# Twelve wide slabs multiplied without splitting, x loaded behind six modulation units, six warming products per sum

## What is computed

```
mod = c_act @ ada_w[l] + ada_b[l]
shift, scl, gate_res = split(mod, 3)
h = rms(x, norm_g[l]) * (1 + scl) + shift
z = h @ w_in            # even layer: 6144 columns u, q, k, v, g; odd layer: more
y = concat(two branches made of z)
x = x + gate_res * ((y * silu(g)) @ w_out[l])
```

## Time and profile before

| | |
|---|---|
| median of 3 runs | 1003.92 us (1001.75 to 1004.96) |
| the profiled execution: its time | 1002.58 us |
| its span, first to last instruction | 1000.8 us |
| mean granted TensorE clock | 0.993 of full speed |
| PE, DVE, ACT busy | 96%, 82%, 42% |
| DMA | 261.31 MB, mean 261 GB/s |
| chain that ended last | PE 85%, DVE 7%, DMA 3%, ACT 2%, issue 2% |

### The profile page before, as it was taken

One profiled execution on the slowest core, in us unless ns is written; L12 is line 12 of the kernel. 1 busy time (PEld: TensorE's weight loads), 2 busy tenths in 40 slices (PEclk: granted clock), 3 DMA queues, 4 the chain that ended last, 5 costly groups with the idle time before them and its releaser, 6 DMA issues.

```text
span 1000.8 us, 19413 instructions
## 1 busy us (share of the span) xinstructions
PE 962.8 (96%) x7328; PEld 931.3 (93%) x7328; DVE 821.0 (82%) x1242; ACT 423.6 (42%) x687; POOL 46.2 (5%) x62
## 2 busy tenths in 40 slices
PE   3799979999999999999999999999999999999998
PEld 3689879999999999999999999999999999998887
DVE  5767887986999779888778899888999996888964
ACT  2210135434555444433435444444446555743331
POOL 1000000020110000000000000000010100000000
PEclk9999899999999999999999999999999999999999
DMA  9999979888876878999957655544445455587962
GB/s 363 396 390 359 348 239 339 326 300 332 303 282 230 288 261 299 339 350 351 327 180 273 229 182 193 187 142 154 155 162 174 159 187 191 195 314 272 375 218 81
DMA packets 71525, 261.31 MB, mean 261 GB/s; under 512 B 7952, under 2 KB 8592, under 8 KB 71200
## 3 DMA queue, kind: packets, MB, share of 16 engines
q1 hardware_dynamic: 66240, 240.90, 66.4%
q10 hardware_dynamic: 2880, 10.49, 2.7%
q0 software_dynamic: 2336, 8.98, 2.5%
HBM read 256.07 MB, written 4.19 MB: 260 GB/s over the span
## 4 chain that ended last, share of the span: by engine, by line
PE 85%; DVE 7%; DMA 3%; ACT 2%; issue 2%; SPq 0%; ACTq 0%; DVEq 0%
PE bank L752 17%; PE bank L753 16%; PE bank L754 16%; PE bank L808 6%; PE bank L773 6%; PE bank L890 3%; PE bank L892 3%; PE bank L893 3%; PE bank L771 3%; DVE wlo L1110 3%; PE bank L821 2%; DVE acc L1120 2%; PE bank L842 2%; PE bank L739 1%; DMA X<-xT 1%
## 5 line engine op out<-in xcount | busy, mean ns | idle before, releaser
L434 ACT ACTIVATE whi<-raw 128x1024 fp32r<-128x1024 f32 x264 | 278.2, 1060 | 419.7 <-PE bank L754 296.6
L1110 DVE TENSOR_TENSOR wlo<-raw,whi 128x1024 fp32r<-128x1024 f32 x264 | 319.7, 1223 | 85.3 <-ACT whi L434 84.1
L752 PE MATMUL bank<-hhi,whi 128*128 128x256 f32 x1168 | 337.1, 289 | 2.2 <-ACT T L664 0.9
L753 PE MATMUL bank<-hlo,whi 128*128 128x256 f32 x1168 | 330.4, 283 | 0.0
L754 PE MATMUL bank<-hhi,wlo 128*128 128x256 f32 x1168 | 330.3, 283 | 0.0
L752 PEld LDWEIGHTS bank<-hhi,whi 128*128 128x128 f32 x1168 | 223.9, 192 | 5.5 <-issue 3.8
L753 PEld LDWEIGHTS bank<-hlo,whi 128*128 128x128 f32 x1168 | 224.0, 192 | 0.1
L754 PEld LDWEIGHTS bank<-hhi,wlo 128*128 128x128 f32 x1168 | 223.9, 192 | 0.0
L1120 DVE SCALAR_TENSOR_TENSOR acc<-ada,cact,acc 128x1024 f32<-128x1024 f32 x152 | 195.2, 1284 | 19.1 <-DMA ada<-ada_units 7.4
L1330 DVE SCALAR_TENSOR_TENSOR Y<-U,par,Y 128x256 f32<-128x256 f32 x240 | 98.5, 478 | 0.0
L773 PE MATMUL bank<-both_g,whi 128*128 128x512 f32 x256 | 89.9, 398 | 0.1
(11 more groups left out here) (186 smaller groups left out, 1314.8 us busy)
## 6 DMA issues: line engine op xcount, KB each, us to landing
raw<-w_slabs SPq DMA_DIRECT2D x262, 512.0 KB, 4.7
ada<-ada_units SPq DMA_DIRECT2D x160, 512.0 KB, 6.7
raw<-w_slabs ACTq DMA_DIRECT2D x20, 512.0 KB, 7.5
V<-ada_units SPq DMA_DIRECT2D x16, 512.0 KB, 11.5
Y<-ada_units SPq DMA_DIRECT2D x16, 512.0 KB, 10.9
X<-xT SPq DMA_DIRECT2D x1, 2048.0 KB, 12.4
x_dram<-X POOLq DMA_DIRECT2D x4, 512.0 KB, 6.3
outT<-X POOLq DMA_DIRECT2D x3, 512.0 KB, 6.1
```

The lines of the kernel that those rows point to most:

```text
L434: act.activation(whi[:, slot], raw[:, slot], ACT.Copy).then_inc(hi_done, 1)
L752: mm(out, whi[:, s, k, :], ahi[:, c, :], start=(c == 0), stop=False)
L753: mm(out, whi[:, s, k, :], alo[:, c, :], start=False, stop=False)
L1110: dve.tensor_tensor(wlo[:, s], raw[:, s], whi[:, s].bitcast(F32), ALU.subtract)\
```

## The change

- `UNSPLIT` becomes 12: chunks 12 to 15 go through `unsplit_chunk` too. `hi` and `lo` of slabs 9, 10 and 11 are gone, and `full_h` makes h for chunks 12 to 15.
- Before a sum there is no warming. After each sum (and after the spread) come 6 products of `keep_warm`, also before chunk 14.
- The spread of the root comes after the sum of piece 0. DVE adds all 16 units of piece 0 before `rsqrt`; ACT loads its table for the root early (`warm(ACT.Sqrt)`) and issues slabs 0 and 1 behind `root`.
- x is issued behind six units instead of four.
- Slab 12 has no place in `raw`: SP loads it into Y (`load_spare`) when all 64 units are added. Behind it SP issues units 64 and 65, slab 14, slab 13, and units 66 to 69.
- DVE's work between the half units of piece 3 is in another order.

```diff
-UNSPLIT = 9
+UNSPLIT = WIDE[0]
...
+        def spare_half(half):
+            return Y[:, 4 * half:4 * half + 4, :].rearrange("p a (b n) -> p (a b) n", n=P)
+
+        def load_spare(eng):
+            eng.wait_ge(ada_done, FIRST + 4)
+            for half in range(2):
+                eng.dma_start(spare_half(half), w_slabs[UNSPLIT:UNSPLIT + 1, :, 8 * half:8 * half + 8, :]
+                              .rearrange("a p k n -> p (a k) n")).then_inc(y_in[half], 16)
+
         def load_slab(eng, w, t):
             for half in range(2):
                 slot = half_slot(w, half)
-                if w >= UNSPLIT + 2:
+                if w == UNSPLIT + 2:
+                    eng.wait_ge(pe_half, 2 * (w - 2) + half + 1)
+                    eng.sem_inc(raw_in[slot], 16)
+                elif w > UNSPLIT:
                     eng.wait_ge(lo_done, 2 * now(w, t) + half + 1)
+                    if w == UNSPLIT + 1:
+                        eng.wait_ge(pe_half, 2 * w + half + 1)
                 elif w >= 2:
                     eng.wait_ge(pe_half, 2 * w + half + 1)
...
-            load_units(0, 4, None)
+            load_units(0, 6, None)
             sp.dma_start(X[:], xT).then_inc(x_in, 16)
-            load_units(4, FIRST - 4, None)
+            load_units(6, FIRST - 6, None)
+            load_slab(sp, UNSPLIT - 2, None)
+            load_slab(sp, UNSPLIT - 1, None)
+            load_spare(sp)
+            load_units(*units_at(10), None)
+            load_slab(sp, UNSPLIT + 2, None)
             load_slab(sp, UNSPLIT + 1, None)
-            load_slab(sp, UNSPLIT + 2, None)
+            load_units(*units_at(11), None)
+            load_units(*units_at(12), None)
...
+            act.wait_ge(const, 1)
+            warm(ACT.Sqrt)
             act.wait_ge(x_in, 16)
             for j in range(KC):
                 square_x(j, j)
+            root(0, QT)
+            act.wait_ge(ada_in[unit_slot(12)], 16 * unit_uses(12, None))
             load_slab(act, 0, None)
             load_slab(act, 1, None)
-            root(0, QT)
...
-            hi(9, None)
-            upper_h(0, range(12, 14))
-            hi(10, None)
-            upper_h(0, range(14, 16))
-            hi(11, None)
+            full_h(range(12, 14))
+            full_h(range(14, 16))
             hi(12, None)
...
-            spread_token(0)
 
             for p in range(3):
                 if p:
-                    pe.wait_ge(ada_done, UNITS * p + 12 + 4)
-                    keep_warm(14, M)
                     pe.wait_ge(ada_done, UNITS * p + 14 + 4)
-                    keep_warm(10, M)
                 reduce_piece(p)
+                if p == 0:
+                    spread_token(0)
+                keep_warm(6, M)
                 for c in range(GROUP * p, GROUP * (p + 1)):
...
-            wide_chunk(0, U0, 12)
-            wide_chunk(0, U0, 13)
+            unsplit_chunk(12)
+            unsplit_chunk(13)
             pe.wait_ge(ada_done, UNITS * 4 + 4)
             for j in range(4, HC):
                 reduce_part(3, j)
-            wide_chunk(0, U0, 14)
-            wide_chunk(0, U0, 15)
+            keep_warm(6, M)
+            unsplit_chunk(14)
+            unsplit_chunk(15)
...
-            add_units(0, 14, None)
+            add_units(0, 16, None)
             dve.wait_ge(stat_done, KC)
             rsqrt(0, QT, M[:, 0:QT], D_MODEL)
             token_diag()
-            add_units(14, 2, None)
...
-            half_units(56, 4)
-            lo(9, None)
+            half_units(56, 2)
             first_half()
-            half_units(60, 2)
-            lo(10, None)
-            half_units(62, 2)
+            half_units(58, 6)
             keep_piece(3, first=4)
             make_gain(0, 3, h0=1)
             make_h(0, range(14, 16))
-            lo(11, None)
```

More of the change, by code:

```diff
@@ L160, in build @@
         raw_in = [sem(f"raw_in{i}") for i in range(4)]
+        y_in = [sem(f"y_in{i}") for i in range(2)]
         ada_in = [sem(f"ada_in{i}") for i in range(8)]
@@ L301, in step @@
                 load_units(*units_at(w), t)
-            for w0, w1 in ((10, 34), (34, 48), (48, 62), (62, 72), (72, 110), (110, 125), (125, 131),
+            for w0, w1 in ((13, 14), (14, 34), (34, 48), (48, 62), (62, 72), (72, 110), (110, 125), (125, 131),
                            (131, 132), (132, N_SLABS - AHEAD)):
-                if w0 in (34, 62, 110, 131):
+                if w0 in (13, 34, 62, 110, 131):
                     for w in range(w0, w1):
@@ L430, in hi @@
                     slot = half_slot(w, half)
+                    if w == UNSPLIT:
+                        act.wait_ge(y_in[half], 16)
+                        act.activation(whi[:, slot], spare_half(half), ACT.Copy).then_inc(hi_done, 1)
+                        continue
                     act.wait_ge(raw_in[slot], 16 * half_uses(w, half, t))
@@ L807, in unsplit_chunk @@
                         pe.wait_ge(raw_in[slot], 16 * half_uses(0, half, None))
-                    last = mm(wide(s), raw[:, slot, k, :], X[:, c, :], start=(c == 0 and s % 2 == 0), stop=False,
+                    last = mm(wide(s), raw[:, slot, k, :], X[:, c, :], start=(c == 0 and s % 2 == 0), stop=(c == KC - 1),
                               skip_group_check=True)
@@ L1109, in lo @@
                     dve.wait_ge(hi_done, 2 * now(w, t) + half + 1)
-                    dve.tensor_tensor(wlo[:, s], raw[:, s], whi[:, s].bitcast(F32), ALU.subtract)\
+                    source = spare_half(half) if w == UNSPLIT else raw[:, s]
+                    dve.tensor_tensor(wlo[:, s], source, whi[:, s].bitcast(F32), ALU.subtract)\
                         .then_inc(lo_done, 1)
@@ L1193, in lower_h @@
                 dve.wait_ge(hhi_done, KC * layer + j + 1)
-                if layer == 0 and j < 12:
+                if layer == 0:
                     dve.tensor_tensor(hlo[:, j, :], X[:, j, :], hhi[:, j, :].bitcast(F32), ALU.subtract)\
```

## The result

| | before | changed |
|---|---|---|
| median | 1002.13 us (6 runs, 1001.09 to 1004.96) | 996.90 us (6 runs, 994.86 to 998.95) |
| ratio, 95% interval | 1 | 0.9934 [0.992, 0.9948] |
| profiled span | 1000.8 us | 993.9 us |
| own time of the profiled execution | 1002.58 us | 995.73 us |

What follows compares the result with a forecast made beforehand. PE, busy 96% of the span, was taken as the bound. Along its chain the cumulative shift was -4.5 at sum 1, -6.4 after chunk 15, -4.9 at slab 13: 1002.58 - 4.9 = 997.7, as median 999.0; range 994.5 to 1003.8 us.

Steps and rivals of the forecast that it cites:

- The start: Up to chunk 0: PE starts it at 41.0 us against 40.80, so the start gives nothing.
- Sum 1: Sum of piece 1, ahead of chunk 4: it starts at 64.2 us instead of 68.70, -4.5.
- Sum 2: Sum of piece 2, ahead of chunk 8: set by data, it starts at 94.2 us against 99.72.
- Wide slabs: Products of chunks 12 to 15: they end at 146.9 us against 153.3, -6.4.
- Slab 13's wait: Slab 13's late load holds up ACT's copies: PE starts slab 13 at 157.0 us against 161.92, -4.9.
- rival 2: Every burst behind a wait starts at half clock: -0.5 us in all, 1003.4, no change; chance 0.17.
- rival 1: The six products behind each sum hold the clock during the wait: -8.3 us in all, 995.6; chance 0.22.
- (3): Units don't come sooner, as DMA doesn't close its 3.5 us hole: -1.4 us, 1002.5, no change; chance 0.04.
- (4): Without products before sums the clock stays at half 10.2 us at each place: 15.5 us more, 1014.5; chance 0.07.

Runs made afterwards that it cites:

- e1: Changed kernel with the 14 and 10 warming products put back ahead of the sums of pieces 1 and 2; ratio to before 0.9962, 997.86 us.
- e8: Changed kernel with DVE adding only 512 of 1024 columns of each unit of pieces 1 and 2 (times only); ratio to before 0.9929.
- e2: Kernel before with only the warming exchanged: none ahead of sums, six products behind each and ahead of chunk 14; ratio to before 0.9930.
- e6: Changed kernel with ACT's rounding of slab 13's second half moved behind the twelve copies of the wide sums; ratio to before 0.9920.
- e11: Kernel before with the warming exchange and 24 filling products ahead of the sum of piece 2; ratio to before 0.9944.
- e3: Changed kernel without any warming products, ahead of or behind the sums; ratio to before 0.9920 over 10 runs.
- e9: Changed kernel with 24 products ahead of the sum of piece 2 and slab 13's second-half rounding behind the twelve copies; ratio to before 0.9877, 992.32 us.
- e4: Changed kernel with slabs 0 and 1 issued by ACT ahead of the root, as before; ratio to before 0.9902.
- e7: Changed kernel with 16 warming products between chunk 7 and the sum of piece 2; ratio to before 0.9928.
- e12: Changed kernel with 24 warming products between chunk 7 and the sum of piece 2; ratio to before 0.9921.
- e10: Changed kernel with 24 products ahead of piece 2's sum, slab 13's second-half rounding behind the copies, slabs 0 and 1 ahead of the root; 0.9896, 992.85 us.

## Why the prediction was right, and where it was off

**The start** (41.0): right, 40.53, with the first slab half as PE's releaser, as forecast, but with some luck. Slabs 0 and 1 were issued at 32.3 and not at 33.6, and the first half took 8.1 us to land and not 6.8: the two errors cancel.

**Sum 1** (-4.5): -5.1. I had DVE's adds at 64.0 as before. They ended at 59.35 + 2.67 = 62.0, and the end of chunk 3 set the sum. More data may account for 1.3 of these 2 us, by the sum that follows. Two windows of the kernel before:

```profile
30.00:64.00 34.00, 27.99 (x122) 24.62 (x123) 27.82 (x36) 5.46 (x11) 0.95 (x1) 1.00 1.00 394
82.00:96.20 14.20, 14.20 (x76) 12.70 (x75) 11.09 (x9) 0.00 (x0) 0.00 (x0) 1.00 1.00 398
```

I had counted only the hole at 73 to 82, 1.42 MB. Between 30 and 64 us before also lacked (410 - 394) x 34 = 0.54 MB, 1.3 us, and between 82 and 96.2 another 12 x 14.2 = 0.17 MB, 0.4 us. The changed kernel holds 409 GB/s from 30 us to 90.8. That more data bring the adds forward is argued and not shown: in e1 the same 409 GB/s from 30 to 64 us left DVE's last add at 62.83 + 1.28 = 64.1, behind a transfer.

**Sum 2** (-5.5): -7.6. This is the term that was mis-sized, for that reason: 3.5 + 1.3 + 0.4 = 5.2 us of transfers come back, not 3.5, and the last add moved from 96.25 to 90.78, 5.5 us, where I had the unit land at 92.8. e8 shows that it is data and not DVE; e2 that the old order of units does as well. That PE would idle 4 us there and the clock would fall was right (4.18 us, then 6.9 at 0.51). I priced the sum at 3.58 and one stretch of 3.4 us in the chunks (17.5); it was 2.91 and 16.73, with the stretch lying partly over the sum and the six products. Chunk 8 stands at 97.64 for 99.4.

**Wide slabs** (-6.4): -9.7. From the end of chunk 11 (120.3) to the end of chunk 15 (143.6) it took 23.3 us for my 23.9. So this term only carries on what came before it: chunk 11 ended 7.7 us early, not 5.0.

**Slab 13's wait**: 10.4 us from the wide end to slab 13, forecast 10.1, with ACT's `hi(13)` as the culprit, which e6 shows by moving it. -8.0 for -4.9.

**The step that failed** is that nothing is lost behind slab 13's wait: the forecast starts slab 13 at 157.0, takes the shift there as the shift of the end, and puts the half clock behind that wait at nothing; only rival 2 charges it, 1.7 us. I took the 3.06 us of idleness at 127.98 with full clock behind as evidence that a wait alone does no harm. The kernel before itself spoke against that: its third half-clock stretch, at 143.4, stands behind 2.10 us of waiting, and I had counted two. e2's 3.26 us at the place of 127.98 ended at half clock (6.8 us from 121.1), e11's 4.84 were followed by 3.4. One exception in one execution was no rule; the changed kernel lost 1.7 us at 154.4, which turned -8.0 into -6.4 at the next large sum (starts 257.3 against 263.7) and -6.8 near the end (the last pair of the last sum starts at 953.8 against 960.6). The two errors had opposite signs, and the second hid half of the first: that the forecast came so near is partly luck. The range's lower end was also 0.2 too low, as rival 1's 995.6 less the 0.9 of a quick load is 994.7 and not 994.5.

**The rivals.** (1) did not happen: the clock fell at sum 2 in spite of the six products, and e3 shows that they do not matter for the time. (2) was right at two places of three (sum 2, slab 13) and wrong at sum 3 (131.44: 1.58 us for 12 products, full clock), where PE had not idled. The Trainium skill, "TensorE: Matmul & The Clock Gate", section "HAM oscillation — how this bites in real kernels", has each burst behind a long wait begin throttled; it says so of a kernel whose waits were 3 to 5 us long, which the prediction left out. Here the trace agrees at 92 (4.18 us) and not at 127.98 of the kernel before, whose 3.06 us are at the short end of those. What the page's case does not cover are the short waits: at 154 there were only 0.90 us of idleness and one-column products ahead. e9, where PE waits nowhere in this part for longer than 1.4 us, has a single stretch of 3.4 us. (3) and (4) are refuted by 409 GB/s and, for the changed kernel, by its longest stretch, 6.8 us; the 10.2 us of rival 4 do occur, once each in e4 and e6.

## What to carry to other kernels

Warming that stands on the path costs its own length: sum 1 came 5.1 us sooner without 5.4 us of it, and taking it away is worth the whole gain in the kernel before (e2). Remove the costs of a chain together: filling the wait for data (e7, e12) or moving slab 13's second half (e6) alone gave 0.06% to 0.14% against the changed kernel, with intervals that overlap, while both gave 0.57% (e9) and both with e4's edit 0.38% (e10). In the profiled executions of e6 and e12 the clock was lost at the other wait. How many filling products are best was not tested: e9's outlast the data by some 2 us. And sum up what a DMA hole gives back over all stretches below the ceiling, not only over the deepest; for the last add of piece 2 that sum (5.2 us) came out near the 5.5 measured.

## What the runs showed of the hardware

In these profiled executions the granted clock falls in stretches of 3.4, 6.8 or 10.2 us. Their number differs between executions of one kernel, as its mean clock does (0.994 to 0.998 in e12's six). Runs of one kernel differ by much more than what is asked (e3's ten span 9.2 us, e1's nine 8.0), and one profiled execution shows one draw of them. The clock is not all of it: in e1's nine the mean clock is 0.996 to 0.998, too little for 8.0 us, and what else differs stays open. Sixteen one-column products tell the clock at a glance, 1.84 us at full and 3.58 at half.

The record of the clock misses the start. From 32 to 44 us the windows say 1.00, yet sum 0 takes 3.57 us, as at half, and the first products of chunk 0 run slowly too. The window of the changed kernel, then of e1, which had no DMA wait ahead of chunk 0:

```profile
40.50:44.00 3.50, 3.47 (x8) 2.86 (x9) 3.50 (x7) 1.86 (x4) 0.00 (x0) 1.00 1.03 411
```

```profile
39.40:44.00 4.60, 4.59 (x22) 4.08 (x22) 4.60 (x8) 2.61 (x6) 0.00 (x0) 1.00 1.03 410
```

8 products in 3.5 us against 22 in 4.6. Chunks 0 to 3 took 20.96 us in e1, e6 and e7, and 23.20 in the changed kernel. e6 and e7 had the same wait of about 1.1 us, so the wait is not the reason. The trace's own record of the clock tells what is: it has no entry before about 39 to 45 us, where the windows print 1.00 for want of one, and its first entry, at full clock, comes at different times. It comes at 45.1 us in the changed kernel, 4.6 us behind the start of chunk 0 (40.53), and at 39.1, 40.3 and 40.5 in e1, e6 and e7, before chunk 0 starts there. Half of 4.6 us is 2.3, and 23.20 less 20.96 is 2.24. The kernel before fits too: first entry at 44.3, chunk 0 at 40.80 and 22.70 us for the four chunks, which is 1.75 by the one reckoning and 1.74 by the other. So PE most likely ran at half clock up to the first entry, at a cost of up to 2.3 us in these chunks that no window shows. Why the first entry comes at different times stays open.
